# Third layer's projections in pairs of seven quarter products, spread over the levels of the recurrence

## What is computed

```
def hgrn2_mixer(h, w_in, lb, norm_w, w_out):
    proj = h @ w_in                                  # 1024 x 4096: q, f, i (values), g
    q = silu(proj[..., :fd])
    f_t = lb + (1.0 - lb) * sigmoid(f)
    log_f = log(maximum(f_t, F_FLOOR))
    k = (1.0 - lb) * sigmoid(-f)
    o = hgrn2_chunkwise(q, k, log_f, i)              # 8 heads of 128
    o = head_rmsnorm(o, norm_w) * silu(g)
    return o @ w_out
```

## Time and profile before

| | |
|---|---|
| median of 3 runs | 2115.74 us (2115.35 to 2116.35) |
| the profiled execution | 2122.56 us, span 2120.9 us |
| TensorE (PE) busy | 2073.4 us, 98% |
| VectorE (DVE) | 800.1 us, 38% |
| ScalarE (ACT) | 552.6 us, 26% |
| GpSimd (POOL) | 362.8 us, 17% |
| `stage_h`, from its first matmul to the end of the last level | 1106.1 to 1432.8 us |

### The profile page before, as it was taken

How to read it: one execution, slowest core, us unless ns; L and a number is a source line. 1 busy time by engine, 2 the same in 40 slices (tenths; PEclk the granted TensorE clock), 3 DMA queues, 4 the chain that set the end, 5 groups by cost and what they waited for, 6 DMA issues and landing times. The chain is left out here.

```text
span 2120.9 us, 26699 instructions
## 1 busy us (share of the span) xinstructions
PE 2073.4 (98%) x10582; PEld 1568.8 (74%) x10582; DVE 800.1 (38%) x1152; ACT 552.6 (26%) x987; POOL 362.8 (17%) x334
## 2 busy tenths in 40 slices
PE   8999999999999999999999999999999999999997
PEld 5444445666554888888876767674899999999996
DVE  2675384446553444436233365563300000000013
ACT  1221012434422111110026575751211111111111
POOL 2000030000003334444332333341110000000011
PEclk9999996999999999999999999999999999999998
DMA  9312550111103565641122111110676586778883
GB/s 340 115 60 94 214 171 10 60 50 50 56 24 109 177 204 206 205 174 72 65 80 70 50 60 50 54 36 1 182 285 213 175 287 223 238 260 301 323 319 152
DMA packets 81388, 308.39 MB, mean 145 GB/s; under 512 B 9848, under 2 KB 10368, under 8 KB 81136
## 3 DMA queue, kind: packets, MB, share of 16 engines
q1 hardware_dynamic: 71280, 275.81, 38.3%
q0 software_dynamic: 6432, 22.11, 2.9%
q10 hardware_dynamic: 3552, 8.74, 1.2%
HBM read 297.30 MB, written 9.33 MB: 145 GB/s over the span
## 5 line engine op out<-in xcount | busy, mean ns | idle before, releaser
L2444 PE MATMUL banks<-sb_act,sb_ring 128*128 128x192 f32 (+3 forms) x3696 | 500.9, 298 | 1.9 <-DMA sb_ring<-in_w_moe_up 1.0
L2444 PEld LDWEIGHTS banks<-sb_act,sb_ring 128*128 128x128 f32 x3696 | 498.3, 191 | 3.0 <-DMA sb_ring<-in_w_moe_up 1.6
L252 PE MATMUL banks<-sb_x_norm,sb_ring 128*128 128x512 f32 x624 | 281.5, 605 | 2.0 <-ACT sb_x_norm L410 2.0
L252 PEld LDWEIGHTS banks<-sb_x_norm,sb_ring 128*128 128x128 f32 x624 | 118.2, 194 | 138.6 <-issue 136.9
L2728 DVE TENSOR_TENSOR sb_act<-sb_work,banks 128x128 f32<-128x128 f32 (+3 forms) x88 | 27.7, 315 | 504.9 <-PE banks L2444 504.6
L252 PE MATMUL banks<-sb_x_res,sb_ring 128*128 128x512 f32 x448 | 194.4, 593 | 0.0
L252 PEld LDWEIGHTS banks<-sb_x_res,sb_ring 128*128 128x128 f32 x448 | 84.7, 190 | 104.8 <-issue 104.8
L263 PEld LDWEIGHTS banks<-sb_ring,sb_x_norm 128*128 128x128 f32 x1024 | 117.6, 194 | 2.5 <-issue 2.4
L263 PE MATMUL banks<-sb_ring,sb_x_norm 128*128 128x128 f32 x1024 | 118.7, 278 | 0.0
L1143 PE MATMUL banks<-sb_act,sb_ring 128*128 128x512 f32 x256 | 112.4, 594 | 0.4 <-DVE sb_act L2099 0.4
L2553 ACT ACTIVATE sb_work<-banks 128x128 f32<-128x128 f32 (+3 forms) x88 | 26.3, 299 | 307.3 <-PE banks L2444 306.3
(11 more groups left out here) (440 smaller groups left out, 2694.0 us busy)
## 6 DMA issues: line engine op xcount, KB each, us to landing
sb_ring<-in_w_moe_up SPq DMA_DIRECT2D x176, 512.0 KB, 4.7
sb_ring<-in_w_moe_down SPq DMA_DIRECT2D x64, 704.0 KB, 5.8
sb_act<-in_cond_w SPq DMA_DIRECT2D x72, 512.0 KB, 4.0
sb_ring<-in_w_ffn_up SPq DMA_DIRECT2D x44, 512.0 KB, 5.2
sb_ring<-in_w_h_in SPq DMA_DIRECT2D x32, 512.0 KB, 3.6
sb_ring<-in_w_in SPq DMA_DIRECT2D x28, 512.0 KB, 3.7
sb_ring<-in_w_m_in SPq DMA_DIRECT2D x24, 512.0 KB, 3.6
sb_ring<-in_w_ffn_down SPq DMA_DIRECT2D x16, 704.0 KB, 5.5
```

The source lines that it names most:

```text
L252: last = m.nc.tensor.matmul(bank[:, 0:act.shape[2]], w[:, rows(k, P)], act[:, k, :], start=(k == 0), stop=(k == kt - 1))
L2444: last = nc.tensor.matmul(ps[:, b % BANKS, 0:cap], w, act, start=(k == 0), stop=(k == kt - 1))
```

## The change

Four blocks (f0, q0, f1 and now g0) stay as they are. The other 28 are made as 14 pairs, 98 quarter products, by a class `Pairs` that is written after the FFN's scheme. `H_BESIDE` is now a list of numbers: so many products stand beside each level, 13 in each of heads 0 to 6 and 7 in head 7. Pairs of values are made with the tokens as rows, 8 matmuls of 128 columns a product.

```
+H_FIRST = [("f", 0), ("q", 0), ("f", 1), ("g", 0)]
+H_PAIRS = [(("f", 2), ("q", 1)), (("v", 0), ("v", 1)), (("f", 3), ("q", 2)), (("v", 2), ("v", 3)), (("f", 4), ("q", 3)),
+           (("g", 1), ("g", 2)), (("f", 5), ("q", 4)), (("v", 4), ("v", 5)), (("f", 6), ("q", 5)), (("g", 3), ("g", 4)),
+           (("f", 7), ("q", 6)), (("v", 6), ("v", 7)), (("g", 5), ("q", 7)), (("g", 6), ("g", 7))]
+H_BESIDE = [[2, 2, 2, 1, 2, 1, 1, 2]] * (HEADS - 1) + [[1, 1, 1, 1, 1, 2, 0, 0]]
...
+    pairs = Pairs(m, plan, len(H_FIRST), len(H_PAIRS), m.HN,
+                  [halves(t) for t in (W[:, 2:4, :], W[:, 4:6, :], W[:, 6:8, :], m.spare[:])],
+                  lambda j: tuple(ps[:, bank, 0:HALF] for bank in ((0, 1, 7), (7, 1, 0))[j % 2]), False,
+                  tokens=[j for j, pair in enumerate(H_PAIRS) if pair[0][0] == "v"])
```

ACT makes the four copies (`keep`, behind the decays of the next level) and takes a finished pair, for (f, q) with a silu table, two halves, a sigmoid table and two full sigmoids:

```
+            def take_pair(j):
+                (kind_a, h_a), (kind_b, h_b) = H_PAIRS[j]
+                a, b = tiles(j)
+                act.wait_ge(m.blocks_done, pairs.blocks_no(j))
+                act.wait_ge(m.added, pairs.added_no(j, C21))
+                if kind_b == "v":
+                    nc.scalar.activation(b[:, LO], pairs.banks(j)[0], ACT.Copy).then_inc(m.evac, 2)
+                    return
+                step(nc.scalar.activation(b[:, LO], pairs.banks(j)[0], ACT.Silu))
+                step(nc.scalar.activation(b[:, HI], b[:, HI], ACT.Silu))
+                if kind_a == "f":
+                    step(nc.scalar.activation(k_of(h_a), a, ACT.Sigmoid, scale=-1.0))
+                    nc.scalar.activation(a, a, ACT.Sigmoid).then_inc(m.evac, 2)
+                else:
+                    nc.scalar.activation(a, a, ACT.Silu).then_inc(m.evac, 2)
```

```
-    norms = [Norm(m, A[:, h:h + 1, :], m.ones128[:], H[:, 6:7, :], H[:, 7, :], m.c("eps6"), False, bank=6)
+    norms = [Norm(m, A[:, h:h + 1, :], m.ones128[:], H[:, 6:7, :], H[:, 7, :], m.c("eps6"), False, bank=5)
...
-    EARLY, OUT_BESIDE = 6, {4: 0, 6: 1}
+    EARLY, OUT_BESIDE = 6, {6: 0, 7: 1}
...
-                    if j in H_BESIDE[h]:
-                        project(*H_BESIDE[h][j])
+                    pairs.multiply(pe, H_BESIDE[h][j])
...
-                        pe.wait_ge(m.evac, plan.done + plan.n - 1 + b)
+                        pe.wait_ge(m.evac, plan.done + plan.n)
```

More of the change, by code:

```diff
@@ L171, in __init__ @@
         self.stored = self.sem("stored")
+        self.products, self.partials, self.combined, self.inputs, self.added = (self.sem("pair_" + n) for n in (
+            "products", "partials", "weights_combined", "inputs_combined", "parts_added"))
+        self.past = {n: 0 for n in ("products", "partials", "combined", "inputs", "added")}
     def sb(self, name, shape, dt=F32):
@@ L266, in by_tokens, with multiply, multiply_tokens @@
     return block
+HALF, HK = S // 2, KD // 2
+LO, HI = slice(0, HALF), slice(HALF, S)
+P1, P7, P6, P2, P5, P4, P3 = range(1, 8)
+T1, T3, T2, T4 = range(1, 5)
+S3, S1, S2, S4 = range(1, 5)
+C11, C22, C21 = range(1, 4)
+def multiply(m, out, n, lhs, rhs, onto=False):
+    for k in range(n):
+        last = m.nc.tensor.matmul(out, lhs(k), rhs(k), start=(k == 0 and not onto), stop=(k == n - 1),
+                                  skip_group_check=onto)
+    return last
+def multiply_tokens(m, out, n, weights, act, onto=False):
+    for t in range(2):
+        for k in range(n):
+            last = m.nc.tensor.matmul(out[:, rows(t, P)], act(k)[:, rows(t, P)], weights(k),
+                                      start=(t == 0 and k == 0 and not onto), stop=(k == n - 1),
+                                      skip_group_check=(onto or t > 0))
+    return last
@@ new lines, in combine_inputs @@
+def combine_inputs(m, eng, engine, act, sums, base, only=None):
+    a11, a12, a21, a22 = act[:, 0:HK, LO], act[:, HK:, LO], act[:, 0:HK, HI], act[:, HK:, HI]
+    s1, s2, s3, s4 = sums
+    made = lambda a, b, out, op, n: give(eng, engine.tensor_tensor(out, a, b, op), m.inputs, base + n)
+    if only in (None, S3):
+        made(a11, a21, s3, ALU.subtract, S3)
+    if only in (None, S1):
+        made(a21, a22, s1, ALU.add, S1)
+    if only in (None, S2):
+        made(s1, a11, s2, ALU.subtract, S2)
+    if only in (None, S4):
+        made(a12, s2, s4, ALU.subtract, S4)
@@ L1454, in _ @@
             norm_out.invert(m, dve)
[L1457 to L1466, removed]
 def stage_ffn(m):
@@ L1870, in products @@
                 last.then_inc(cross_done, 1)
-            for kind, h in H_BLOCKS[0:4]:
+            for kind, h in H_FIRST:
                 project(kind, h)
@@ L2039, in diff, with combine @@
                                                    ALU.subtract), t_ready, n)
+            def combine(h, j):
+                which = {P1: T1, P7: T3, P6: T2, P5: T4}
+                for n, i in beside(h, j):
+                    if i + 1 in which and n + 1 < pairs.n:
+                        pairs.combine(pool, n + 1, which[i + 1])
             m.glink.on(pool)(nc.gpsimd.memset(H[:, 4:6, :], 0.0))
+            pool.wait_ge(m.hn_ready, norm.scaled + KD)
+            combine_inputs(m, pool, nc.gpsimd, m.HN, pairs.sums, pairs.past["inputs"])
+            for which in (T1, T3, T2, T4):
+                pairs.combine(pool, 0, which)
             diff(0, 1)
@@ L2107, in times, with add @@
                                                   ALU.mult), q_ready, n)
+            def add(h, j):
+                which = {P2: C11, P5: C22, P4: C21}
+                for n, i in beside(h, j):
+                    if i + 1 in which:
+                        pairs.add(dve, n, which[i + 1], tiles(n))
             norm.scale_tiles(m, dve)
```

260 lines of the change are left out of this document (222 added, 38 removed).

## The result

The changed kernel takes 2142.73 us (median of 4 runs, 2134.22 to 2145.20) against 2116.05 for the kernel before on the same chip: ratio 1.0108, 95% interval 1.0086 to 1.0129. It is **slower by some 23 us** by that ratio (the two medians are 26.7 us apart), where 2110 was forecast and 2124 was the range's end. The profiled execution took 2144.33 us, span 2142.6.

The account below looks back on a forecast made before the run. TensorE was taken as the bound, with slack on the others. -24.9 (TensorE) + 20.8 - 1.8 (waits) + 0.2 (hold) = -5.7 us, giving a median of 2110; range for 8 in 10 from 2097 to 2124.

Parts of the forecast that it names:

- 0.2 (hold): DVE's instructions between SBUF tiles last longer while POOL works; 0.2 us added to the sum.
- What bounds the kernel: Third layer's heads: TensorE is the bound, busy 98% of the span, with slack on the other engines.
- TensorE loses 24.9: Quarter products replace blocks: ten pairs by features save 17.7 us, four of values 7.2, 24.9 us less.
- The walk, ACT's part: Head 3 laid out instruction by instruction: ACT's own chain of 18.6 us ends decay 4 at 17.5.
- The walk, DVE's part and the hold at its low end: Head 3: times 5 ends at 24.45, level 5 starts at 24.55; POOL's hold on DVE taken at its low bound, nothing.
- The high end: Upper bound of POOL's hold: 0.46 us for each of seven DVE instructions, decay 4 to times 6; 3.2 us a head.
- Waits 20.8: TensorE's added waits over the eight heads, 20.8 us, less the 1.8 there before.
- TensorE's granted clock still 1.00: In the stage from 1136 on, TensorE stays at the 2.4 GHz level, with some 20 us of waits.
- DVE held by POOL, slower: Rival: hold from decay 4 to times 6 in heads 2 to 6, 2.4 us a head, +6.3, 2122; chance 0.24.
- TensorE sets the pace: Rival: the walk is too strict, ACT and DVE run ahead; 2091 to 2104, say 2098; chance 0.2.
- The hand-walk: Heads laid out with every instruction in its order and durations from rows; waits added 20.8 us.

Follow-up runs that it names:

- Experiment 1: Changed kernel, but POOL's four weight combinations of each of pairs 4 to 13 work on 8 of 512 elements; ratio 1.0062 to the kernel before.
- experiment 7: Changed kernel; the first pair's first product waits only for the third block's take, the fourth's wait stands before the second product; ratio 1.0097 to before.
- Experiments 3: Changed kernel with the matmuls of level 4 issued three times over in heads 2 to 6; ratio 1.0122 to the kernel before.
- 13 to 15: Kernel before, TensorE waiting ahead of cross blocks of heads 1 to 5 for one, two or three useless POOL instructions; 2127.2, 2144.0, 2156.5 us against 2117.7.
- experiment 11: Changed kernel with another table of products and other places for finish, logs, decay 6 and sums; ratio 0.9924 to the kernel before, 2102.48 us.
- experiment 9: Changed kernel with experiment 7's wait and another table of how many products stand beside each level; ratio 0.9948 to the kernel before.
- experiment 4: Changed kernel with one of the two products beside level 1 moved to beside level 5 in heads 0 to 6; ratio 1.0136 to the kernel before.
- experiment 5: Changed kernel with DVE's times of level 5 put straight behind the take of level 3; ratio 1.0146 to the kernel before.

## Why the prediction was wrong, step by step

Its sum was -24.9 (TensorE) + 20.8 - 1.8 (waits) + 0.2 (hold) = -5.7. Measured in the stage: +23.3.

- **What bounds the kernel**: right for the kernel before, and the question, how much slack of the others the change uses up, was the right one.
- **TensorE loses 24.9**: too much. A product stands at 1.73 us behind another (1.79 for values), but at 1.78 to 1.84 behind a level, and there are far more such changes now: the 56 products that stand behind something else are together 4.6 us longer than by that price. The gain is some 20 us. It agrees with what is left over: the stage's 319.4 us less 27.6 of waits and 16.6 of clock are 275, where the kernel before had 294 (the forecast's own heads were 30.8 + 7 x 33.9 = 268). Head 1, with no wait and clock 1.00, took 34.7, not 33.9.
- **The walk, ACT's part**: right to 0.1 us (decay 4 of head 3 ends 17.6 us from the start, 17.5 was forecast).
- **The walk, DVE's part and the hold at its low end**: this failed first. Times 5 ended at 26.1, not 24.45. "I take the low end, since after times 4 POOL ... is done before the cross decays start" named the wrong victim: the cross decays did run at 0.56 us, but the second half of finish, between them and times 4, lost 0.87, the first half 0.69, times 4 0.35. The high end, 0.46 us an instruction, was too low as well. Level 5 of head 3 was 1.6 us late. Experiment 1 gives 1.4 of it back. DVE's instruction ended 0.28 us after POOL's. By the exclusive lock of the Trainium skill ("SBUF — State Buffer", "SBUF: two separate sides") it would stand still until POOL's instruction is over, and the trace agrees but for 0.20 us: 0.28 and not its own 0.48 us were left to it then.
- **Waits 20.8**: 27.6. By head 2.3, 0.2, 3.2, 0.9, 1.3, 3.2, 3.1 and 6.6 us were forecast and 4.4, 0, 4.3, 2.0, 2.5, 3.5, 6.3 and 4.8 measured, so the total also hides an error the other way in head 7. A wait I missed is the first pair's for g0's take (2.12 us, experiment 7).
- **"TensorE's granted clock still 1.00"**: **the step that failed by most.** I priced a wait at its own length. Behind most waits of 2 to 4 us the clock was at 1.2 GHz for a time, which cost 16.6 us over the stage. With it the items close: -20 for TensorE, +27.6 - 1.8 of waits, +16.6 of clock, +22.4 of the 23.3 measured. Without it they are +5.8: the hold, the missed wait and TensorE's smaller gain had already turned the sign, but 5.8 is within the stated range; the clock made it 22. Experiments 3 and 13 to 15 show the clock's part from both sides.
- **Rivals.** "DVE held by POOL, slower" came nearest, with the right place and sign (+6.3), and only the smaller part of the price: experiment 1, which takes the combinations' part of the hold away from head 2 on, gives 10 us back, clock included. "TensorE sets the pace" is wrong for this table and nearer the truth in experiment 11, where 8 us of waits are left.
- The hand-walk took the table as given. It didn't ask what another order of the same work would do, which was worth some 39 us (1.0108 to 0.9924).

## What to carry to other kernels

When a change removes work from the engine that bounds the kernel, price each new wait of TensorE at its length, plus 2 to 3 us if it is 2 us or longer (an upper price around 2 us, see below), and look at the granted clock and at an instruction of known length behind it. If a change that removes work loses, count the waits before giving it up: one moved instruction moved the wait to the next step here, while the order of a whole stage, rearranged at once, turned +1.1% into -0.8%. On DVE, look at which two-input SBUF instructions start while POOL works, not at how busy POOL is in the neighbourhood.

## What was not expected of the hardware

- Whether TensorE waits in one piece or in two mattered more than how long it waited in all: two waits of 0.86 and 1.31 us left the clock at 1.00 (head 4 of experiment 1), one of 2.48 us cost 3.2 us on top.
- The fall isn't fixed by the wait's length. In experiment 9 a wait of 2.01 us had no effect (cross blocks behind it 1.56 us); in 11 one of 1.70 had (2.31). The first of five equal waits of 1.32 us was followed by a fall, the others were not. Over the heads in all the traces of this case, a fall of the granted clock came in the 7 us behind 1 of 28 waits of 1.0 to 1.4 us, 5 of 27 of 1.45 to 1.95, 20 of 28 of 2.0 to 2.2, and 48 of 51 longer ones (2.41 and 2.63 us in experiment 4 and 3.50 in experiment 5 had none). What else decides it stays open.
- With the same 2.5 us wait before level 5 of head 4, the head took 40.3 us in the changed kernel and 38.6 in experiment 7, clocks 0.92 and 0.96: how long the clock stays down varies too.
